# Splitting the mLSTM's state products by head and double-buffering its logits and scores

## What is computed

```python
def mlstm_chunk_outputs(q, k, v, ig, lf, starts):
    ...
    s = jnp.einsum('bhcjd,bhcsd->bhcjs', q, k) * d
    num = jnp.einsum('bhcjs,bhcsv->bhcjv', s, v) + a[..., None] * jnp.einsum('bhcvd,bhcjd->bhcjv', c0, q)
    den = jnp.sum(s, axis=-1) + a * jnp.einsum('bhcd,bhcjd->bhcj', n0, q)
    return num / jnp.maximum(jnp.abs(den), jnp.exp(-m))[..., None]
```

## Time and profile before

| | us |
|---|---|
| median of three runs | 2765.07 |
| lowest and highest of them | 2760.31, 2766.59 |
| the profiled execution (the lowest) | 2760.31 |
| its span | 2758.5 |
| TensorE busy in the span | 2454.7 (89%) |
| VectorE busy | 1513.6 (55%) |
| ScalarE busy | 956.7 (35%) |
| GpSimd busy | 1125.4 (41%) |

### The profile page before, as it was taken

The page is one execution under the profiler, slowest core; times in us unless marked ns, Lnnn a source line. Parts: engine busy times, 40 slices in busy tenths (PEclk is TensorE's granted clock), DMA queues, the critical chain, the costliest instruction groups (busy, mean ns, idle before and its releaser), DMA issues.

```text
span 2758.5 us, 31907 instructions
## 1 busy us (share of the span) xinstructions
PE 2454.7 (89%) x11622; PEld 1975.0 (72%) x11622; DVE 1513.6 (55%) x2034; ACT 956.7 (35%) x1494; POOL 1125.4 (41%) x843
## 2 busy tenths in 40 slices
PE   5999768899999997679989999897878788899999
PEld 5888657788888886556768888676534465688887
DVE  6756756755555544988552122479379444452523
ACT  3312222512121224457552233443333343432322
POOL 1433003344444432358634444345764131344444
PEclk6999879999999998889999999999989899999999
DMA  5333103232333331321122323132200020232323
GB/s 223 115 102 127 39 8 115 84 114 101 112 111 102 114 99 39 102 54 41 56 77 92 99 92 96 62 108 84 92 0 0 31 73 27 69 107 91 99 92 107
DMA packets 68821, 231.68 MB, mean 84 GB/s; under 512 B 8048, under 2 KB 10992, under 8 KB 68592
## 3 DMA queue, kind: packets, MB, share of 16 engines
q1 hardware_dynamic: 68720, 230.35, 25.8%
HBM read 219.57 MB, written 2.10 MB: 80 GB/s over the span
## 4 chain that ended last, share of the span: by engine, by line
PE 57%; issue 15%; DVE 13%; POOL 10%; ACT 3%; DMA 1%; SPq 0%; POOLq 0%; DVEq 0%; ACTq 0%
PE PS L640 41%; POOL HL L517 9%; PE PS L658 6%; DVE RD L2242 2%; PE PS L677 1%; PE PS L609 1%; PE PS L901 1%; DVE ZZ L2396 1%; DVE SM L2226 1%; PE PS L1160 1%; PE PS L783 1%; PE PS L1042 1%; PE PS L1077 1%; DVE STATE L2081 1%; PE PS L786 1%
## 5 line engine op out<-in xcount | busy, mean ns | idle before, releaser
L517 POOL TENSOR_TENSOR HL<-RAW,HL 128x512 fp32r<-128x512 f32 x614 | 905.0, 1497 | 1502.3 <-ACT HL L1205 1502.0
L640 PE MATMUL PS<-HA,HL 128*128 128x512 f32 (+1 forms) x2592 | 557.3, 368 | 18.3 <-DVE V L2007 5.1
L640 PE MATMUL PS<-HID,HL 128*128 128x512 f32 (+1 forms) x2832 | 565.6, 362 | 0.0
L640 PE MATMUL PS<-HB,HL 128*128 128x512 f32 (+1 forms) x2592 | 542.8, 362 | 0.0
L640 PEld LDWEIGHTS PS<-HID,HL 128*128 128x128 f32 x2832 | 478.8, 188 | 85.4
L640 PEld LDWEIGHTS PS<-HA,HL 128*128 128x128 f32 x2592 | 444.4, 190 | 111.4 <-issue 32.3
L640 PEld LDWEIGHTS PS<-HB,HL 128*128 128x128 f32 x2592 | 442.8, 189 | 77.5
L1205 ACT ACTIVATE HL<-RAW 128x1024 fp32r<-128x1024 f32 x307 | 323.0, 1053 | 495.5 <-PE PS L640 385.5
L1859 DVE CUSTOM_DVE_ANT_0 ADJ<-ADA,CB 128x1024 f32<-128x1024 f32 x160 | 267.8, 1674 | 8.8 <-DVE X L1781 2.7
L1781 DVE SCALAR_TENSOR_TENSOR X<-PS,MOD,X 128x256 f32<-128x256 f32 (+1 forms) x120 | 75.7, 658 | 335.2 <-PE PS L640 317.1
L658 PE MATMUL PS<-HA,HL 128*128 128x256 f32 (+1 forms) x576 | 136.1, 399 | 69.6 <-DVE HA L1762 49.2
(11 more groups left out here) (372 smaller groups left out, 2779.1 us busy)
## 6 DMA issues: line engine op xcount, KB each, us to landing
RAW<-wstream SPq DMA_DIRECT2D x307, 512.0 KB, 3.5
ADA<-adastream SPq DMA_DIRECT2D x80, 512.0 KB, 3.6
EARLY<-adastream SPq DMA_DIRECT2D x16, 512.0 KB, 14.4
QB<-QH SPq DMA_DIRECT2D x32, 128.0 KB, 2.3
X<-x_in SPq DMA_DIRECT2D x8, 384.0 KB, 6.8
QC<-QL SPq DMA_DIRECT2D x16, 128.0 KB, 2.3
out<-X SPq DMA_DIRECT2D x8, 256.0 KB, 2.3
X<-mem SPq DMA_DIRECT2D x1, 1024.0 KB, 12.3
```

The source lines that it names most:

```text
L517: a = pool.tensor_tensor(HL[:, t % RING, 1, half], RAW[:, t % RAW_RING, half], HL[:, t % RING, 0, half].bitcast(F32), ALU.subtract)
L640: mm = pe.matmul(bank(t % 2, r), w[:, wp, k * P:(k + 1) * P], a[:, ap, lo:hi], start=(k == 0 and (wp, ap) == (0, 0)), stop=(k == nk - 1 an ...
```

## The change

- `sums(n)` goes head by head. Each head has DT times V1 (128 rows), then QW times the state with the head's own 64 rows (`CST8[p]`, 129 columns), added to it, then KW times V1 with the head's own 64 columns of weights, written to 64 partitions of PSUM. No product with zeros is left, and heads with the same `h % 2` share a bank.
- The state is one tensor `CST8` with the head's parity on the partition halves, so `state(n)` is two instructions on 128 partitions. What the chunk contributes stands in banks 4 and 5 behind the numerators (columns 258 to 386).
- The exponents go to bank 0 or 1 by the parity of n, and wait for the decay of step n-2. The scores go to one half or the other of banks 2 and 3. The selector products go to bank 6 and stand ahead of the wait for `masked`; the scores keep that wait.
- One memset instead of two at the start; `JUNK`, the unused output of the squares, moves to another place; index orders follow.

```diff
@@ -250,9 +250,8 @@
         DT = sb("DT", [P, 2, ML_HEADS, P], offset=hb_at + 12288)
         QW = sb("QW", [P, 2, 2, P], offset=hb_at + 16384)
         KW = sb("KW", [P, 2, ML_HEADS, 64], offset=hb_at + 18432)
-        STATE = [sb("STATE0", [P, 2, 2 * (ML_DV + 1)], offset=hb_at + 20480),
-                 sb("STATE1", [P, 2, 2 * (ML_DV + 1)], offset=arena + 67840)]
-        JUNK = sb("JUNK", [P, ML_HEADS, P], offset=arena + 12288)
+        CST8 = sb("CST8", [P, 2, 2, ML_DV + 1], offset=hb_at + 20480)
+        JUNK = sb("JUNK", [P, ML_HEADS, P], offset=arena + 67840)
         SEL = [sb("SEL0", [100, ML_HEADS, 64], F32R, offset=rows_at + 1536),
                sb("SEL1", [100, ML_HEADS, 64], F32R, offset=hb_at + 22560)]
 
@@ -406,9 +405,7 @@
             return PS[:, 4:6, 0:2 * (ML_DV + 1)].rearrange("p b (h n) -> p b h n", n=ML_DV + 1)
 
         def two(x):
-            return x.rearrange("p (b h) -> p b h", b=2)
-
-        STATE_BANK = (1, 6)
+            return x.rearrange("p (h b) -> p b h", b=2)
 
         block = stack.enter_context(nc.Block())
 
@@ -742,9 +739,9 @@
 
                 def decay_and_scores(n):
                     d, b = ML_STEPS[n]
-                    if n:
-                        pe.wait_ge(S("decay"), n)
-                    dst = PS[:, 0, :]
+                    if n >= 2:
+                        pe.wait_ge(S("decay"), n - 1)
+                    dst = PS[:, n % 2, :]
                     pe.matmul(by_head(dst), NIDR[:, :], MASKR[:, d, :].unsqueeze(1).to_broadcast([P, ML_HEADS, P]),
                               start=True, stop=True)
                     pe.matmul(by_head(dst), A8[:, tok(b)], T8R[0:100, d, :].unsqueeze(2).to_broadcast([100, ML_HEADS, P]),
@@ -753,19 +750,18 @@
                         mm = pe.matmul(dst[:, h * P:(h + 1) * P], T8N[0:100, d, h:h + 1].to_broadcast([100, P]),
                                        M8[:, tok(b)], start=False, stop=True, skip_group_check=True)
                     mm.then_inc(S("exponents"), 1)
-                    if n:
-                        pe.wait_ge(S("masked"), n)
                     if n >= 2:
-                        if n > 2:
-                            pe.wait_ge(S("q_weighted"), n - 2)
+                        pe.wait_ge(S("q_weighted"), n - 2)
                         if n == 3:
                             pe.wait_ge(S("act_once"), ACT_ONCE["sel_set"])
                         for c in range(2):
-                            pe.matmul(PS[:, 2 + c, 2 * P:3 * P], SEL[d][:, 2 * c:2 * c + 2, :].rearrange("p h n -> p (h n)"),
+                            pe.matmul(PS[:, 6, c * P:(c + 1) * P], SEL[d][:, 2 * c:2 * c + 2, :].rearrange("p h n -> p (h n)"),
                                       E8[:, tok(b)], start=True, stop=True)
+                    if n:
+                        pe.wait_ge(S("masked"), n)
                     for h in range(ML_HEADS):
                         p = slice(64 * (h % 2), 64 * (h % 2) + 64)
-                        mm = pe.matmul(PS[:, 2 + h % 2, h // 2 * P:(h // 2 + 1) * P], KT[p, h // 2, tok(b)], QT[p, h // 2, tok(b)],
+                        mm = pe.matmul(PS[:, 2 + h % 2, (2 * (n % 2) + h // 2) * P:(2 * (n % 2) + h // 2 + 1) * P], KT[p, h // 2, tok(b)], QT[p, h // 2, tok(b)],
                                        start=True, stop=True)
                     mm.then_inc(S("scores"), 1)
 
@@ -775,19 +771,16 @@
                     if n:
                         pe.wait_ge(S("num_read"), n)
                         pe.wait_ge(S("state_new"), states_until(n))
-                    for c in range(2):
-                        pair = slice(2 * c, 2 * c + 2)
-                        dst = PS[:, 4 + c, 0:2 * (ML_DV + 1)]
-                        values = V1[:, b, pair, :].rearrange("p h n -> p (h n)")
+                    for h in range(ML_HEADS):
+                        p = slice(64 * (h % 2), 64 * (h % 2) + 64)
+                        o = h // 2 * (ML_DV + 1)
+                        dst = PS[:, 4 + h % 2, o:o + ML_DV + 1]
+                        mm = pe.matmul(dst, DT[:, n % 2, h, :], V1[:, b, h, :], start=True, stop=(n < 2))
                         if n >= 2:
-                            pe.matmul(dst, QW[:, n % 2, c, :], STATE[d][:, c, :], start=True, stop=True)
-                        for i in range(2):
-                            o = slice(i * (ML_DV + 1), (i + 1) * (ML_DV + 1))
-                            mm = pe.matmul(dst[:, o], DT[:, n % 2, 2 * c + i, :], V1[:, b, 2 * c + i, :], start=(n < 2),
-                                           stop=True, skip_group_check=(n >= 2))
+                            mm = pe.matmul(dst, QW[p, n % 2, h // 2, :], CST8[p, d, h // 2, :], start=False, stop=True)
                         if WITH_STATE[n]:
-                            mm = pe.matmul(PS[:, STATE_BANK[c], 0:2 * (ML_DV + 1)],
-                                           KW[:, n % 2, pair, :].rearrange("p h n -> p (h n)"), values, start=True, stop=True)
+                            mm = pe.matmul(PS[p, 4 + h // 2, 258:387], KW[:, n % 2, h, :], V1[:, b, h, :],
+                                           start=True, stop=True)
                     mm.then_inc(S("summed"), 1)
 
                 def turn(i):
@@ -1368,13 +1361,13 @@
                 act.wait_ge(S("exponents"), n + 1)
                 if n >= 2:
                     act.wait_ge(S("summed"), n - 1)
-                act.activation(DT[:, n % 2, :, :], by_head(PS[:, 0, :]), ACT.Exp).then_inc(S("decay"), 1)
+                act.activation(DT[:, n % 2, :, :], by_head(PS[:, n % 2, :]), ACT.Exp).then_inc(S("decay"), 1)
 
             def first_half(n):
                 d, b = ML_STEPS[n]
                 act.wait_ge(S("inverse"), n + 1)
                 for h in range(ML_HEADS):
-                    a = act.activation(HS[:, b, h, :], numerators()[:, h // 2, h % 2, 0:ML_DV], ACT.Copy,
+                    a = act.activation(HS[:, b, h, :], numerators()[:, h % 2, h // 2, 0:ML_DV], ACT.Copy,
                                        scale=REC[:, n % 2, h:h + 1])
                 a.then_inc(S("num_read"), 1)
 
@@ -2061,14 +2054,14 @@
                     dve.wait_ge(S("summed"), n - 1)
                     dve.wait_ge(S("scores"), n + 1)
                     dve.tensor_tensor(QW[:, n % 2, :, :], QT[:, :, tok(b)],
-                                      PS[:, 2:4, 2 * P:3 * P], ALU.mult).then_inc(S("q_weighted"), 1)
+                                      PS[:, 6, 0:2 * P].rearrange("p (c n) -> p c n", c=2), ALU.mult).then_inc(S("q_weighted"), 1)
                 if WITH_STATE[n]:
                     dve.tensor_tensor(KW[:, n % 2, :, :], KTOK[:, b, :, :],
                                       EK[:, b, d, :].unsqueeze(2).to_broadcast([P, ML_HEADS, 64]), ALU.mult)
                 dve.wait_ge(S("scores"), n + 1)
                 dve.wait_ge(S("decay"), n + 1)
                 w = DT[:, n % 2, :, :].rearrange("p (h b) n -> p b h n", b=2)
-                s = PS[:, 2:4, 0:2 * P].rearrange("p b (h n) -> p b h n", n=P)
+                s = PS[:, 2:4, 256 * (n % 2):256 * (n % 2) + 256].rearrange("p b (h n) -> p b h n", n=P)
                 dve.tensor_tensor(w, w, s, ALU.mult).then_inc(S("masked"), 1)
 
             def state(n):
@@ -2076,10 +2069,8 @@
                 dve.wait_ge(S("summed"), n + 1)
                 if WITH_STATE[n]:
                     for c in range(2):
-                        for i in range(2):
-                            p, o = slice(64 * i, 64 * i + 64), slice(i * (ML_DV + 1), (i + 1) * (ML_DV + 1))
-                            a = dve.scalar_tensor_tensor(STATE[d][p, c, o], STATE[d][p, c, o], RHO[p, d, c, b:b + 1],
-                                                         PS[p, STATE_BANK[c], o], ALU.mult, ALU.add)
+                        a = dve.scalar_tensor_tensor(CST8[:, d, c, :], CST8[:, d, c, :], RHO[:, d, c, b:b + 1],
+                                                     PS[:, 4 + c, 258:387], ALU.mult, ALU.add)
                     a.then_inc(S("state_new"), 1)
 
             def inverse(n):
@@ -2096,7 +2087,7 @@
                 dve.wait_ge(S("inverse"), n + 1)
                 dve.wait_ge(S("num_read"), n)
                 for h in range(ML_HEADS):
-                    a = dve.scalar_tensor_tensor(HS[:, b, h, :], numerators()[:, h // 2, h % 2, 0:ML_DV],
+                    a = dve.scalar_tensor_tensor(HS[:, b, h, :], numerators()[:, h % 2, h // 2, 0:ML_DV],
                                                  REC[:, n % 2, h:h + 1], HS[:, b, h, :], ALU.mult, ALU.add)
                 a.then_inc(S("num_read"), 1)
 
@@ -2125,10 +2116,7 @@
                                   ALU.subtract).then_inc(S("conv_lo"), 1)
 
             dve.wait_ge(S("tile_done"), 25)
-            dve.wait_ge(S("ada_done"), 2 * (40 - ADA_PE))
-            for d in range(2):
-                a = dve.memset(STATE[d][:, :, :], 0.0)
-            link(a)
+            link(dve.memset(CST8[:, :, :, :], 0.0))
             for s in range(N_ML + 3):
```

## The result

| | before | changed |
|---|---|---|
| median of the timed runs, us | 2763.8 (4 runs, 2760.3 to 2766.6) | 2806.6 (4 runs, 2802.5 to 2808.2) |
| ratio | | 1.0152, 95% interval 1.0137 to 1.0168 |
| profiled execution, us | 2760.3 | 2791.7 |

Slower, as forecast, but by 42.8 us where I had forecast 15, and outside the range that I gave (2767 to 2795).

A forecast was written before the change was run, and what follows sets the result against it. Bound: a chain of short dependent pieces in the mLSTM steps, no engine full. 20.0 + 2.5 - 7.2 - 0.3 = +15.0 us takes the profiled 2760.3 to 2775.3; forecast 2780 as the median lies 4.8 higher, range 2767 to 2795.

The forecast's parts named there:

- The chain of the kernel before: mLSTM step: 6.22 us of sums, state, inverse and numerators in sequence, nothing overlapping, no engine full.
- The price of a change of shape: Sums: array drains at tile shape changes, 0.15 us into 64 columns, 0.2 out, 0.2 to QW; together 20.0 us more.
- the cover: Next step's exponents and scores run off the chain with 1.6 us to spare, shrinking to some 0.7 us.
- The same at the lower clock: Shape changes in the 38% of the stage at 1.2 GHz cost 0 to 7.6 us more, taken as 2.5.
- the clock falls: Rival: emptied array makes the five fast steps also run at 1.2 GHz; 2795 us, chance 0.14.
- State update, -7.2 us: VectorE state update: two instructions for four, saving 0.72 us on the chain in each of ten steps.
- Buffers, 0: Double-buffered logits and scores, selector product moved to bank 6: 0 to 0.3 us, taken as 0.
- Memset, -0.3: Stage start: one of two 0.49 us memsets goes, worth 0 to 0.5 us, taken as 0.3.
- Shapes cost nothing: Rival: shape changes in the sums are free, so the state updates decide; 2757.5 us, faster, chance 0.06.
- only 64 columns free: Rival: only the 64-column shape is free, leaving two paid changes a head; +10 us, 2775, chance 0.15.
- 64-row products side by side: Rival: the eight QW passes overlap in different array halves, saving 4.3 us over ten steps; 2776 us, chance 0.03.
- What would show it wrong: Passes following at 0.11 us across shape changes, or a granted stage clock outside 0.75 to 0.87.

The follow-up runs named there:

- full_array_flags: Changed kernel with QW and KW zero-padded to the whole 128x128 array, no shape changes, flags set so every product is added; 2755.7 us, 0.9972 of before.
- grouped_flags: Changed kernel's 24 products reordered as four DT, four QW, four KW, flags set so every product is added; 2745.2 us, 0.9942 of before.
- cols_only: Changed kernel with QW padded to the whole array, KW still in 64 columns; 2771.3 us, 1.0030 of before.
- grouped: Changed kernel's products reordered as four DT, four QW, four KW; its flags lose the DT products of heads 0 and 1; 2747.4 us, 0.9947 of before.
- grouped_one_half: grouped_flags with the four QW products in head order 0, 2, 1, 3; 2750.2 us, 0.9947 of before.

## Why the prediction was wrong

*The chain of the kernel before*: right; full_array_flags and grouped_flags shortened its plain fast step of 6.2 us to 5.3 and 4.8, by what they took out of it.

*The price of a change of shape*: right at full clock. 0.35 for the way into 64 columns and back, measured in sums(0) and in cols_only. The step 0 grew from 1.68 to 3.14 us (1.2 predicted, 1.46 measured up to the next exponents, which takes in the way out that I had left to the cover). The Trainium skill's sentence on the drain, in TensorEngine Tiling (Array Packing), Key Properties, has these rows on its side; the earlier trace rows, where none shows, stay unexplained.

*"The same at the lower clock", 2.5 us*: this is the step that failed. I took the clock of before, 38% of the stage at 1.2 GHz, as given and only asked what a change costs at it. The price itself was inside my bounds: a head of 2.08 us less six passes of 0.215 leaves 0.79 us for its three changes, against 0.55 at full clock and at most twice that. But the changed kernel runs its stage from 312 us on, 127 us, at 1.2 GHz. That the clock was a result of the change, and not a circumstance, I had only as a rival, "the clock falls", with 0.14. It was the right one, priced at 2795 where 2806.6 came out. I charged it only for five fast sums of 2.2 us and up to 4 of drains. The sums of such a step grew from 2.9 to 8.3 us, and the exponents and scores from 2.1 to 3.5.

*The cover, "some 0.7 us, still above zero"*: failed with it. At full clock it about holds: cols_only idles 0.48 us ahead of its sums (361.08). At 1.2 GHz the 3.5 us of exponents and scores no longer fit behind the 2.4 us of VectorE and ScalarE (382.70 to 385.07), so they are on the chain. That made TensorE the whole chain, and the sum had two parts that can't stand together: a saving on VectorE and a longer TensorE that hides VectorE.

*State update, -7.2 us*: the count and the length of one were right (20 of 346 ns), the saving too small: 0.53 us from the update to `inverse` for 1.47, so 0.94 a step and not 0.72, or 9.4 for ten. It is worth 4.4 us in the changed kernel, where VectorE mostly waits, and 16.6 in grouped_flags, clock included.

*Buffers, 0*: right in grouped_flags, the one order in which it was tried. *Memset, -0.3*: not tried alone. *Shapes cost nothing*, *only 64 columns free*: both fell, 64 columns pay 0.35 a head in cols_only. *64-row products side by side*: not in the changed order, as said, but in grouped.

*What would show it wrong*: I had named a stage clock outside 0.75 to 0.87. It is 0.56.

The changed kernel's matmuls are in flight for 125.8 of the 146 us, 86%, against 67% in the earlier trace rows. That looks like a busier engine, and is one that does the same columns over more time, at half the clock and with drains between. The Trainium skill warns of just this reading, in Trainium Kernel Development and Optimization, Performance Expectations: matmul busy time is a bad metric for how close a kernel is to its limit, because matmuls are pipelined. The traces agree: with the same 24 passes a step, full_array_flags has matmuls in flight for 64.0 us of its stage, and the changed kernel for 125.8.

## What to carry to other kernels

Where small products alternate in array shape, count the changes and price them from two neighbouring passes in a trace: here 0.15 to 0.2 us each at 2.4 GHz, 0.2 to 0.3 at 1.2. Then ask what the pattern does to the clock before using the clock of the kernel before, because here that was most of the loss. By an estimate: at full clock the changes and the merged update come to 20.0 - 9.4 - 0.3 = 10.3 us, with the price of the prediction and the measured 0.94 a step, and of the stage's 35.7 us some 25 are left for the clock. Sort the same products by shape, with the two halves of the array in one group: the split that lost 43 us in one order gains 16 to 19 in another.

## What the runs showed that I had not expected

- TensorE stayed at 1.2 GHz for 129.7 us on end while matmuls were in flight 86% of the time. The spells of the kernel before last 3.4 to 13.7 us.
- Which shapes alternate, and in which order, counts beside the number of changes: eight changes over 64 rows never got the upper clock back in the stage (its clock 0.55), eight over 64 columns did (0.74), and five with the row halves apart took 78.5 us (0.58) in the profiled run and less in four of twelve.
- TensorE ran eight 64-row passes side by side in 0.65 us even where neighbours in program order used the same half (grouped_one_half).
- Of two profiles of the changed kernel the stretch behind the stage differed by 16.9 us (557.5 and 569.1 in the MLP, 1717.9 and 1724.0 from there on, the rest ahead of the MLP). I have no cause for it.
